# Predicated copies for HGRN's levels, shared evictions and alternating rows in forgetting attention, and one weight load in another place

## What is computed

```python
# HGRN2 (cut): decay is per channel, so a score needs the whole decay between two tokens
scores = jnp.einsum('bhtk,bhsk,bhtsk->bhts', qi, ki, decay)       # decay = exp(b_t - b_s), causal
o = jnp.einsum('bhts,bhsv->bhtv', scores, vi) + jnp.einsum('bhtk,bhkv->bhtv', qi * jnp.exp(bi), state)
# forgetting attention (cut)
sc = jnp.einsum('bqhd,bkhd->bhqk', qi, k) * scale + (ci[..., :, None] - c[:, :, None, :])
sc = jnp.where(pi[:, None] >= kpos[None, :], sc, -jnp.inf)
p = jax.nn.softmax(sc, axis=-1)
o = jnp.einsum('bhqk,bkhd->bqhd', p, v)
# at the end
return _rmsnorm(x, norm_final)
```

## Time and profile before

| | us |
|---|---|
| median of 3 runs | 1307.15 |
| lowest, highest | 1306.17, 1309.4 |
| the profiled execution, its own time | 1307.57 |
| its span in the profile | 1305.7 |
| TensorE busy in the span | 1216.9 (93%) |
| VectorE, ScalarE, GpSimd busy | 480.7, 386.1, 117.0 |

### The profile page before, as it was taken

One profiled execution on the slowest core, in us unless ns is written; L12 is line 12 of the kernel. 1 busy time (PEld: TensorE's weight loads), 2 busy tenths in 40 slices (PEclk: granted clock), 3 DMA queues, 4 the chain that ended last, 5 costly groups with the idle time before them and its releaser, 6 DMA issues.

```text
span 1305.7 us, 17650 instructions
## 1 busy us (share of the span) xinstructions
PE 1216.9 (93%) x7269; PEld 675.6 (52%) x7269; DVE 480.7 (37%) x1123; ACT 386.1 (30%) x745; POOL 117.0 (9%) x129
## 2 busy tenths in 40 slices
PE   7999999999999999997898888788879999999996
PEld 6445744457446898874554444455643333333332
DVE  6344122111996346754512221134531112221216
ACT  5014711114773231136651000366201111111113
POOL 2100022210000000011000000111011111111100
PEclk9999999999999999998999999889769999999999
DMA  7111122220134434203040003401149999999719
GB/s 259 39 63 33 33 77 75 76 67 15 63 116 176 119 79 151 99 1 130 1 161 1 1 0 134 193 33 49 49 170 417 422 421 415 426 413 419 300 50 369
DMA packets 67270, 199.54 MB, mean 153 GB/s; under 512 B 25613, under 2 KB 42225, under 8 KB 56433
## 3 DMA queue, kind: packets, MB, share of 16 engines
q1 hardware_dynamic: 59328, 181.39, 35.9%
q0 software_dynamic: 7808, 16.96, 3.5%
q10 hardware_dynamic: 48, 0.01, 0.0%
HBM read 172.63 MB, written 35.14 MB: 159 GB/s over the span
## 4 chain that ended last, share of the span: by engine, by line
PE 87%; DVE 5%; ACT 3%; issue 2%; DMA 2%; SPq 0%; POOL 0%; DVEq 0%; POOLq 0%; ACTq 0%
PE bank L2348 29%; PE bank L1441 13%; PE bank L1502 7%; PE bank L1467 7%; PE bank L753 2%; PE bank L1557 2%; PE bank L739 2%; PE bank L1517 2%; PE bank L1427 2%; PE bank L2472 2%; PE bank L786 1%; PE bank L814 1%; PE bank L844 1%; DMA arena<-y_d 1%; PE bank L1576 1%
## 5 line engine op out<-in xcount | busy, mean ns | idle before, releaser
L2348 PE MATMUL bank<-arena 128*128 128x512 f32 (+3 forms) x1088 | 378.0, 508 | 0.0
L2348 PEld LDWEIGHTS bank<-arena 128*128 128x128 f32 x1088 | 206.9, 191 | 165.3 <-issue 152.7
L1441 PE MATMUL bank<-arena 128*32 128x512 f32 x1536 | 170.9, 596 | 2.0 <-DVE arena L1204 2.0
L1441 PEld LDWEIGHTS bank<-arena 128*32 128x32 f32 x1536 | 50.8, 111 | 116.8 <-issue 116.8
L1923 ACT ACTIVATE arena<-bank 128x512 f32<-128x512 f32 (+1 forms) x64 | 32.9, 514 | 219.5 <-PE bank L2348 219.2
L1502 PE MATMUL bank<-arena 128*128 128x512 f32 x220 | 95.6, 593 | 0.0
L1467 PE MATMUL bank<-arena 128*32 128x512 f32 x768 | 87.4, 595 | 0.7 <-ACT arena L1113 0.7
L1213 DVE TENSOR_TENSOR arena<-arena,bank 128x256 f32<-128x256 f32 x25 | 10.5, 422 | 168.7 <-ACT arena L1109 148.9
L1911 ACT ACTIVATE arena<-arena 128x1024 f32<-128x1024 f32 x26 | 27.4, 1055 | 135.0 <-DVE arena L1273 106.2
L1502 PEld LDWEIGHTS bank<-arena 128*128 128x128 f32 x220 | 41.4, 190 | 49.7 <-issue 49.7
L1273 DVE TENSOR_TENSOR arena<-arena,bank 128x512 f32<-128x512 f32 x32 | 22.0, 689 | 115.2 <-PE bank L1502 87.8
(11 more groups left out here) (388 smaller groups left out, 1622.4 us busy)
## 6 DMA issues: line engine op xcount, KB each, us to landing
arena<-in_w_e_gu SPq DMA_DIRECT2D x27, 2048.0 KB, 14.7
arena<-in_w_e_dn SPq DMA_DIRECT2D x33, 1024.0 KB, 14.2
arena<-in_w_in SPq DMA_DIRECT2D x11, 1024.0 KB, 5.0
arena<-y_d SPq DMA_DIRECT2D x8, 1024.0 KB, 5.0
arena<-hz_d SPq DMA_DIRECT2D x4, 1792.0 KB, 8.1
arena<-in_w_e_gu SPq DMA_DIRECT2D x6, 1024.0 KB, 9.8
arena<-in_w_e_gu SPq DMA_DIRECT2D x12, 512.0 KB, 13.0
pk_d<-arena SPq DMA_DIRECT2D x8, 640.0 KB, 2.9
```

What stands on the lines that cost most here:

```text
L1441: ins = mm(bank[part, :], hgT[:, k, part], w_gu(es[i] % NB, k), start=(k == 0), stop=(k == KT - 1))
L2348: ins = mm(psum[PROJ_BANKS[u % 3]][0:rows, 0:n], lhs(k), rhs(k), start=(k == 0), stop=(k == KT - 1))
```

## The change

HGRN. The tile `h_pm[it % 2]` now holds, per head, four 128x128 tiles, one for each unit of an iteration. Scores are made level by level: `hgrn_scores(it, lv)` fills one bank per head with the four units of one level. VectorE writes level 0 with a mask product, and each further level with a copy predicated on that level's mask over the same tile, after the copy two before it (the previous level of that head). `hgrn_out(u)` takes one product per head instead of eight; it needs all levels of its iteration, so the outputs of an iteration are issued between levels 4 to 7 of the next.

Attention. The rows come in the order of `FOX_ORDER`. Scores are one row ahead instead of two; the transposes of the first head go ahead of the previous row's values, those of the second behind them. ScalarE computes the next row's exponentials between the evictions of the two heads. The last group of the second head is evicted by VectorE (`fox_rowsT`, its own semaphore `x_pd`), which also copies the reciprocal row itself.

The last norm's weights are loaded into `levT`, on SP behind the loads of experts 1 and 2 (semaphore `t_x2`). ScalarE's square and root for the delta-rule mixer come ahead of all output copies.

```diff
-        h_pm = [view(o, 2, NL + 1, P) for o in (o_g2 + 2 * T, o_ht + 6 * T)]
+        h_pm = [view(o, 2, 4 * P).rearrange("p a (n t) -> p a n t", n=4) for o in (o_g2 + 2 * T, o_ht + 6 * T)]
+        FOX_ORDER = [(i, 0) for i in (4, 0, 7, 1, 6, 2, 5, 3)] + [(i, 1) for i in (7, 2, 6, 3, 5, 1, 4, 0)]
 # act_tail
+            act.wait_ge(s["g_os"], NT)
+            nc.scalar.activation(fin_sq, d_o, ACT.Square).then_inc(s["f_act"], 1)
+            act.wait_ge(s["f_ss"], 1)
+            nc.scalar.activation(fin_ss[:, :], fin_ss[:, :], ACT.Sqrt, bias=epsc[:, 0:1],
+                                 scale=1.0 / HD).then_inc(s["f_act"], 1)
             for u in range(NU):
...
+                act_hgrn_o(act, u)
-            def sums(g):
-                act.wait_ge(s["x_pv"], g + 1)
-                if g >= 2:
-                    act.wait_ge(s["x_o"], g - 1)
-                nc.scalar.activation(x_rb[g % 2], psum[6 + g % 2][:, P:2 * P], ACT.Copy).then_inc(s["x_rs"], 1)
+            def probsT(g, par):
+                i, c = fox_step(g)
+                if par == 0 and g >= 2:
+                    act.wait_ge(s["x_pv"], g - 1)
+                for b in range(fox_halves(g) - par):
+                    m = min(4, i + 1 - 4 * b)
+                    j = group_of(g, par, b)
+                    act.wait_ge(s["x_tr"], j + 1)
+                    nc.scalar.activation(x_pT[g % 2][:, par, 4 * b:4 * b + m, :],
+                                         psum[4 + j % 2][:, 0:m * P].rearrange("p (b q) -> p b q", q=P),
+                                         ACT.Copy).then_inc(s["x_pt"], 1)
+            probs(0)
             for g in range(NS):
-                probs(g)
-                if g >= 1:
-                    sums(g - 1)
-                probsT(g)
+                probsT(g, 0)
+                if g + 1 < NS:
+                    probs(g + 1)
+                probsT(g, 1)
 # dve_tail
-            for u in range(NU):
-                for b in range(2):
-                    for par in range(2):
-                        t = 4 * u + 2 * b + par
-                        dve.wait_ge(s["h_scr"], t + 1)
-                        if t % 4 == 0 and u >= 2:
-                            dve.wait_ge(s["h_o"], u - 1)
-                        v.tensor_tensor(h_pm[u % 2][:, par, 4 * b:4 * b + 4],
-                                        psum[t % 6][:, :].rearrange("p (l t) -> p l t", l=4),
-                                        levT[:, 4 * b:4 * b + 4], ALU.mult).then_inc(s["h_pm"], 1)
-                gdn_finish(u)
+            for t in range(2 * NIT * (NL + 1)):
+                it, lv, par = t // (2 * NL + 2), t // 2 % (NL + 1), t % 2
+                dve.wait_ge(s["h_scr"], t + 1)
+                if lv >= 1:
+                    dve.wait_ge(s["h_pm"], t - 1)
+                if lv == 0 and par == 0 and it >= 2:
+                    dve.wait_ge(s["h_o"], 4 * (it - 1))
+                scores = psum[t % 6][:, :].rearrange("p (n t) -> p n t", n=4)
+                if lv == 0:
+                    v.tensor_tensor(h_pm[it % 2][:, par], scores, bc(levT[:, lv], 1, [P, 4, P]),
+                                    ALU.mult).then_inc(s["h_pm"], 1)
+                else:
+                    v.copy_predicated(h_pm[it % 2][:, par], bc(levT[:, lv].bitcast(i32), 1, [P, 4, P]),
+                                      scores).then_inc(s["h_pm"], 1)
+                if t % 4 == 3:
+                    gdn_finish(t // 4)
             def fox_out(g):
                 i, c = fox_step(g)
-                dve.wait_ge(s["x_rs"], g + 1)
+                dve.wait_ge(s["x_pv"], g + 1)
+                link(v.tensor_copy(x_rb[g % 2], psum[6 + g % 2][:, P:2 * P]))
+            def fox_rowsT(g):
...
+                v.tensor_copy(x_pT[g % 2][:, 1, 4 * b:4 * b + m, :],
+                              psum[4 + j % 2][:, 0:m * P].rearrange("p (b q) -> p b q", q=P)).then_inc(s["x_pd"], 1)
+            for g in range(2):
+                fox_biased(g)
+                gdn_rows(2 * g)
+                gdn_rows(2 * g + 1)
             for g in range(NS):
-                fox_biased(g)
...
+                if 1 <= g < NS - 1:
+                    fox_biased(g + 1)
+                fox_inverse(g)
+                if g >= 1:
+                    fox_out(g - 1)
+                fox_rowsT(g)
 # pe_tail
-                for lv in range(NL + 1):
-                    for par in range(2):
-                        ins = mm(psum[6 + u % 2][rows(par), 0:P], a_i[:, n, hd(2 * c + par)], h_pm[u % 2][:, par, lv],
-                                 start=(lv == 0), stop=(n == 0 and lv == NL))
+                for par in range(2):
+                    ins = mm(psum[6 + u % 2][rows(par), 0:P], a_i[:, n, hd(2 * c + par)], h_pm[it % 2][:, par, n4],
+                             start=True, stop=(n == 0))
-            hgrn_scores(0)
-            for u in range(NU):
-                if u + 1 < NU:
-                    hgrn_scores(u + 1)
-                hgrn_out(u)
+            for it in range(NIT + 1):
+                for lv in range(NL + 1):
+                    if it < NIT:
+                        hgrn_scores(it, lv)
+                    if it >= 1 and lv >= 4:
+                        hgrn_out(4 * (it - 1) + lv - 4)
             for g in range(NS + 1):
-                if g + 2 < NS:
-                    fox_scores(g + 2)
+                if 1 <= g < NS - 1:
+                    fox_scores(g + 1)
+                if g < NS:
+                    fox_transposes(g, 0)
                 if g >= 1:
                     fox_values(g - 1)
                 if g < NS:
-                    fox_transposes(g)
+                    fox_transposes(g, 1)
 # last norm
-        fin_g = view(o_g2 + 4 * D, D)
+        fin_g = levT[:, :, :].rearrange("p a b -> p (a b)")
+            sp.dma_start(fin_g, a["norm_final"].unsqueeze(0).to_broadcast([P, D])).then_inc(s["t_x2"], 16)
-            dve.wait_ge(s["t_rw"], 96)
+            dve.wait_ge(s["t_x2"], 32)
-                if m == 0:
-                    sp.dma_start(fin_g, a["norm_final"].unsqueeze(0).to_broadcast([P, D])).then_inc(s["t_rw"], 16)
```

More of the change, by code:

```diff
@@ L321, in hybrid_trunk, with group_of, group_evicted @@
         L_AT = 3
+        FOX_T = []
+        for g in range(NS):
+            for par in range(2):
+                for b in range(fox_halves(g)):
+                    FOX_T.append((g, par, b, "dve" if par == 1 and b == fox_halves(g) - 1 else "act"))
+            if g == L_AT:
+                FOX_T += [(g, 2, i, "act") for i in range(CT * NHALF)]
+        by = lambda who, j: sum(t[3] == who for t in FOX_T[:j + 1])
+        def group_of(g, par, b):
+            return FOX_T.index((g, par, b, "dve" if par == 1 and b == fox_halves(g) - 1 else "act"))
+        def group_evicted(eng, j):
+            eng.wait_ge(s["x_pt"] if FOX_T[j][3] == "act" else s["x_pd"], by(FOX_T[j][3], j))
         l_xc = view(o_bc + CT * T, CT, T)
```

126 lines of the change are left out of this document (52 added, 74 removed).

## The result

The changed kernel takes 1296.2 us (median of ten runs; 1290.14 to 1302.74), the kernel before 1308.87 in the same session (ten runs; 1306.17 to 1319.78): a ratio of 0.9898, 95% interval [0.9869, 0.9927]. It is faster by 1.0%, and slower than the forecast by 18.5 us. The profiled execution took 1293.63 us, its span is 1291.8.

The account below looks back on a forecast made before the run. TensorE bounds HGRN and waits bound attention; VectorE was to become HGRN's bound. 1307.57 - 16.9 - 11.3 - 1.3 = 1278.1, with the median 0.4 lower: 1277.7 us; range 1266 to 1300, the forecast case's own 1268 to 1288 (0.62).

Parts of the forecast that it names:

- HGRN, -16.9: HGRN stage: VectorE becomes the bound at 47.1 us, copies 0.62 us apart (upper bound 1.22); stage 16.9 us shorter.
- Rival C: HGRN: the predicated copy makes a second pass, 1.22 us, 33.6 us more; kernel slower at 1311 us; chance 0.11.
- D: HGRN: TensorE's new waits let its clock fall; at the low level throughout, 1312 us; chance 0.05.
- Attention, -11.3: Attention stage: 62 us of row pairs, 6.2 of start and 10 of norm, 78.2 for 89.5 us; 11.3 us shorter.
- the norm of HGRN's output: Attention: ScalarE's norm with VectorE's products behind it, allowed 10 us around the row pairs.
- the 6.2 of the start: Attention's start: 6.2 us for 4.7, because the first row has 5 blocks instead of 1.
- the 1.2 of hand-overs: Attention: about six uncovered hand-overs of 0.2 us a pair of rows, half of the 2.8 us before.
- The rates of the rows: Attention: TensorE takes 0.67 us a block, so 72 blocks and 16 rows come to 52 us.
- the 34.5 us that VectorE waited for ScalarE's copy: Attention: VectorE's wait for ScalarE's copy of the reciprocal row, 34.5 us, goes; used as an argument against rival B.
- Rival B: Attention gains nothing because VectorE is now the late one: 1289 us, up to 1296; chance 0.17.
- The end, -1.3: Last stage: without the weights' 0.5 MB load, the next expert-output loads land earlier; 1.3 us shorter, bounds 0 and -2.
- Every stretch between as long as before: Stages between attention and the end: predicted to keep their lengths, no change.

Follow-up runs that it names:

- e9: Changed kernel with scores two rows ahead, HGRN-output norm behind row 0, its VectorE part split over two rows, and idle products in cross-attention: 1279.17 us, ratio 0.9784.
- e13: Changed kernel with attention rows in the old order and scores two rows ahead, shared evictions kept: 1287.44 us.
- e3: Kernel before with only the last norm's weights loaded into levT: 1308.18 us, ratio 1.0008.
- e7: Changed kernel with idle TensorE products in the cross-attention's rows and the router's tail: 1287.48 us, ratio 0.9836.
- e8: Kernel before with idle TensorE products in the cross-attention's rows and the router's tail: 1308.08 us, ratio 0.9999.
- e2: Kernel before with only the attention part of the change: 1310.24 us, ratio 1.0006.
- e4: Changed kernel with 8 idle TensorE products, 6.9 us in all, between attention and the output product: 1303.2 us.
- e1: Kernel before with only the HGRN part of the change: 1294.09 us, ratio 0.99.
- e5: Changed kernel with attention's scores and biased scores two rows ahead instead of one: 1292.76 us, ratio 0.9867.
- e12: Changed kernel with attention rows in the old order, scores still one row ahead: 1290.78 us.

## Why the prediction was wrong

The profiled execution took 1293.6 us for a sum of 1278.1. By the parts of the sum:

- **HGRN, -16.9: right.** -16.2; copies 0.718 long and 0.61 apart, as the lower end. VectorE is the bound, TensorE's new waits for VectorE are 4.4 us and cost nothing. Rival C is refuted: no second pass. Of D there is a little. By stretches of the stage TensorE was granted

```profile
505.00:515.00 10.00, 9.41 (x127) 8.73 (x127) 7.10 (x12) 3.58 (x3) 0.00 (x0) 0.83 0.87 343
515.00:525.00 10.00, 7.70 (x98) 7.06 (x96) 9.87 (x14) 0.57 (x2) 0.00 (x0) 0.83 0.43 159
525.00:535.00 10.00, 8.93 (x134) 7.34 (x132) 9.90 (x16) 0.85 (x4) 0.00 (x0) 1.00 0.66 249
```

  0.83 to 525 us and 1.00 from there. It cost nothing: from its first mask product at 507.81 VectorE had no gap above 0.26 us (9.87 and 9.90 of 10 us busy in the second and third stretch).
- **Attention, -11.3: wrong.** -4.2. The step that failed is the allowance around the steady rows: "the norm of HGRN's output [...] which I leave at 10 us", the 6.2 of the start, and the 1.2 of hand-overs in the first two pairs. By the lengths above they came to 13.2, 7.1 and 2.4 a pair, slower products included. The rates of the rows behind them held. I moved the scores from two rows ahead to one and counted the chain of a pair, but not the norm's blocks in it (7 us on ScalarE, 5 on VectorE), and I priced all of TensorE's work at its full clock. e9 shows the sizes: with the lead back and the norm moved and split the stage is 77.7 us, and of the 7.6 us between the two, 3.3 are TensorE's waits and 4.3 its slower products. That e9 lands on the forecast's 78.2 is no proof of the forecast's chain: it took three edits, and the wait of 2.12 us at the start is still in it. One argument failed with it: the 34.5 us that VectorE waited for ScalarE's copy did go (7.5 us are left, now for TensorE's L842), but TensorE's own waits fell by 2.2 us only. Of VectorE's long wait at most the 6.0 us of e13 had held TensorE up. (Nor was it the longest of the stage: GpSimd waited 52.5 us.) Rival B named the right size in part (1289) by a wrong cause: VectorE is not full, it has 54.89 us of work in 85.3.
- **The end, -1.3: right.** -0.7 in this pair of executions; over all, 31.0 us on average in the twelve profiled kernels with the new place and 32.5 in the five without, -1.5 (31.6 and 32.5 where the kernels with fillers are left out). It is too little for the whole time to show (e3).
- **"Every stretch between as long as before": wrong.** +6.7 us in the cross-attention, a term put at nothing. By the granted clock alone: 7.4 us more of TensorE's busy time for the same work, 0.6 less of waits (e7 and e8 confirm it). I had asked of the clock only in the stages that the change touches. The trace of before had shown the risk: 0.83 in the first 40 us of that stage and 0.58 in its last 37.

These are 0.7, 7.1, 0.6 and 6.7 us, with 0.5 in the two stages between: 15.5, but for rounding. The median lies 2.6 us above the profiled execution, and 0.4 of the forecast was the step to the median of before: 18.5 in all.

What stays open: how the attention part makes the long runs frequent. They come with it (5 of 10 runs, e2 6 of 10, e4 5 of 10) and hardly without it (e1, e3, before); the start of the stage is not it (e4), nor the moved load (e2, e3). e13, with shared evictions but the old order and lead, had four runs within 2.3 us and a stage of 138.3, which points at the order or the lead; but four runs are few, and e5 and e12, each with one of the two undone, spread over 6.7 and 9.5 us. I have not found what it is.

## What to carry to other kernels

A gain in one stage is not the gain of the kernel while TensorE's clock in another stage can fall: split each stage's length into TensorE's busy time and the rest, and compare busy times of the same work, before looking for a new wait or crediting an edit with one. When a software pipeline's lead is shortened, price the longest block of foreign work on each engine against the new lead, and put that block where the pipeline waits anyway. A few idle products in the gaps can be faster than the gaps; where the clock is high already they bring nothing (e8).

## What the runs showed of the hardware

A predicated copy of 128x512 f32 from a bank, with an int32 mask from SBUF, takes 718 ns and can start every 0.61 us, like a product of the same shape. Idle products worth 18.9 us of TensorE's time made a kernel 8.7 us faster (e7), since they raised the granted clock in their stage from 0.83 and 0.61 to 0.97 and 0.82. And one and the same stage took 144.0 or 137.8 us (after and e4), 137.3 or 150.0 (before and e2), all by TensorE's busy time for the same work (113.13 and 105.05, 105.78 and 118.80 us); one of these courses repeated to 0.1 us in another kernel (after and e3).
